# A decoder step on one core: cached values become the stationary operand of the probability products

## What is computed

```python
s = (jnp.einsum('bqhd,bqkhd->bhqk', qblk[:, :, g], kg) * scale
     - slopes[g][None, :, None, None] * dist.astype(jnp.float32)[None, None, None, :])
s = jnp.where(valid[None, None], s, NEG_INF)
lse = jax.nn.logsumexp(s, axis=-1)
p = jnp.exp(s - lse[..., None])
outs.append(jnp.einsum('bhqk,bqkhd->bqhd', p, vg))
...
wts = jax.nn.softmax(jnp.stack(lses, axis=0), axis=0)
return jnp.einsum('gbhq,gbqhd->bqhd', wts, jnp.stack(outs, axis=0))
```

## Time and profile before

| what | value |
|---|---|
| median of 3 runs | 940.0 us (938.59 to 940.89) |
| the profiled execution's own time | 937.09 us |
| its span on the core | 935.0 us |
| mean granted PE clock | 0.992 |
| PE busy (with its weight loads: PEld) | 905.9 us, 97% (840.2 us, 90%) |
| DVE, ACT, POOL busy | 556.4, 322.9, 209.7 us |
| stage B, by the trace | from about 405 to 702 us |

### The profile page before, as it was taken

How to read it: one execution, slowest core, us unless ns; L and a number is a source line. 1 busy time by engine, 2 the same in 40 slices (tenths; PEclk the granted TensorE clock), 3 DMA queues, 4 the chain that set the end, 5 groups by cost and what they waited for, 6 DMA issues and landing times.

```text
span 935.0 us, 19353 instructions
## 1 busy us (share of the span) xinstructions
PE 905.9 (97%) x6844; PEld 840.2 (90%) x6844; DVE 556.4 (60%) x1013; ACT 322.9 (35%) x512; POOL 209.7 (22%) x179
## 2 busy tenths in 40 slices
PE   7999999999999999999999999999989999999996
PEld 6998999999999999997887877877759999999996
DVE  4348634863476347656876786786787333333377
ACT  4134403440344034344544453453455222222210
POOL 0037202720272027241123114115110000000003
PEclk8999999999999999999999999999999999999999
DMA  7999799689968996573783693694596978888712
GB/s 214 215 271 325 290 183 268 235 295 181 280 220 294 181 270 233 208 249 110 265 313 132 228 355 123 204 349 154 191 367 210 302 256 262 267 270 286 233 63 102
DMA packets 163819, 221.04 MB, mean 236 GB/s; under 512 B 9088, under 2 KB 136832, under 8 KB 162048
## 3 DMA queue, kind: packets, MB, share of 16 engines
q1 hardware_dynamic: 158944, 207.09, 71.5%
q0 software_dynamic: 4176, 11.02, 3.6%
q10 hardware_dynamic: 656, 2.36, 0.7%
HBM read 207.71 MB, written 100.01 MB: 329 GB/s over the span
## 4 chain that ended last, share of the span: by engine, by line
PE 80%; DVE 10%; issue 4%; DMA 2%; ACT 2%; POOL 0%; DVEq 0%; SPq 0%; POOLq 0%; ACTq 0%
PE bank L757 19%; PE bank L759 19%; PE bank L758 19%; PE bank L1056 6%; PE bank L752 5%; PE bank L787 4%; PE bank L882 2%; DVE wl L1505 2%; PE bank L1101 2%; PE bank L1092 2%; PE bank L1018 1%; DMA xn<-in_x_prompt_dram 1%; DVE part_l L1734 1%; PE bank L1115 1%; PE bank L857 1%
## 5 line engine op out<-in xcount | busy, mean ns | idle before, releaser
L757 PE MATMUL bank<-xh,wh 128*128 128x288 f32 x640 | 191.8, 300 | 3.2 <-DVE vn L1572 3.1
L759 PE MATMUL bank<-xh,wl 128*128 128x288 f32 x640 | 188.7, 295 | 0.0
L758 PE MATMUL bank<-xl,wh 128*128 128x288 f32 x640 | 188.6, 295 | 0.0
L757 PE MATMUL bank<-wh,xh 128*128 128x256 f32 x640 | 184.7, 289 | 0.7 <-DVE qk L1700 0.6
L758 PE MATMUL bank<-wl,xh 128*128 128x256 f32 x640 | 181.0, 283 | 0.0
L759 PE MATMUL bank<-wh,xl 128*128 128x256 f32 x640 | 180.9, 283 | 0.0
L1505 DVE TENSOR_TENSOR wl<-raw,wh 128x1024 fp32r<-128x1024 f32 (+1 forms) x104 | 130.2, 1286 | 14.3 <-ACT wh L1260 13.0
L1260 ACT ACTIVATE wh<-raw 128x1024 fp32r<-128x1024 f32 (+1 forms) x104 | 102.3, 1018 | 79.7 <-PE bank L787 42.2
L757 PEld LDWEIGHTS bank<-wh,xh 128*128 128x128 f32 x640 | 123.0, 192 | 2.5 <-DVE qk L1700 0.8
L757 PEld LDWEIGHTS bank<-xh,wh 128*128 128x128 f32 x640 | 120.2, 188 | 5.2 <-DVE vn L1572 2.6
L758 PEld LDWEIGHTS bank<-wl,xh 128*128 128x128 f32 x640 | 123.1, 192 | 0.6
(11 more groups left out here) (219 smaller groups left out, 1755.5 us busy)
## 6 DMA issues: line engine op xcount, KB each, us to landing
raw<-in_w_in_dram SPq DMA_DIRECT2D x128, 256.0 KB
cslot<-in_cache_kv_w_dram SPq DMA_DIRECT2D x32, 1024.0 KB, 5.9
out_dram<-in_cache_kv_w_dram SPq DMA_DIRECT2D x16, 2040.0 KB, 10.1
out_dram<-in_cache_kv_w_dram SPq DMA_DIRECT2D x32, 1020.0 KB, 10.0
far<-in_cache_kv_w_dram SPq DMA_DIRECT2D x32, 512.0 KB, 10.4
out_dram<-in_cache_kv_w_dram SPq DMA_DIRECT2D x20, 504.0 KB, 10.8
raw<-in_w_in_dram SPq DMA_DIRECT2D x16, 512.0 KB
out_dram<-in_cache_kv_w_dram SPq DMA_DIRECT2D x24, 252.0 KB, 3.1
```

What stands on the lines that cost most here:

```text
L757: pe.matmul(out, lhs[0](k), rhs[0](k), start=(k == 0), stop=False)
L758: pe.matmul(out, lhs[0](k), rhs[1](k), start=False, stop=False)
L759: last = pe.matmul(out, lhs[1](k), rhs[0](k), start=False, stop=(k == n - 1))
```

## The change

1. In `cached_output` the operands change places. For every tile and each of the 4 heads, the tile's 128 x 128 block of that head's values is stationary and 16 columns of `pm` move (8 queries, high and low part, as 2 x 8 with a step of 32): with `part_h` and `part_l` that is 8 matmuls a tile for 2. The output comes out turned: `bank[4]`, 128 rows (head dimension) x 64 columns.
2. ACT's `output_lows`, DVE's `output_sum` and PE's `cached_turn` go. DVE's `output(x)` waits for PE's last tile, copies the 32 low columns to a new tile `osum`, adds the 32 high ones, and multiplies into `oa`. PE waits for `co_read` ahead of the score tiles, not behind them, since they write the bank that `output` reads.
3. On DVE `statistics` of a body stands behind `probs(1)` and the first three value tiles; it stood ahead of `next_projected(0)`.
4. On DVE in stage A, `values(22)` stands ahead of `far_sum(2)`, `far_sum(3)` moves behind `output(1)`, and the later far sums each move back by one place.

```diff
+        osum = sb("osum", [P, ROWS], F32, scope_b)
...
                     pe.wait_ge(qm_done, r * 2 + (x + 1))
                     settle(pe)
+                    pe.wait_ge(co_read, r * 2 + (x + 1))
+                    settle(pe)
                     for j in range(KTILES):
                         if j + 2 < KTILES:
                             transpose_tile(r, x, j + 2)
                         score_tile(j)
-                    pe.wait_ge(co_read, r * 2 + (x + 1))
-                    settle(pe)
...
                         n, probs = (P, pm[:, i * BLK:(i + 1) * BLK]) if i < TILES else (OWN, pn[:, :])
-                        for part in (part_h, part_l):
-                            last = pe.matmul(bank[4][0:BLK, :], probs, part[i % 3][0:n, :],
-                                             start=(i == 0 and part is part_h), stop=(i == TILES and part is part_l))
+                        for h in range(H):
+                            o, q = (a.rearrange("p (s h q) -> p s h q", s=2, h=H)[:, :, h, :] for a in (bank[4][:, 0:BLK], probs))
+                            for part in (part_h, part_l):
+                                last = pe.matmul(o, part[i % 3][0:n, h * DH:(h + 1) * DH], q,
+                                                 start=(i == 0 and h == 0 and part is part_h),
+                                                 stop=(i == TILES and h == H - 1 and part is part_l))
                         last.then_inc(part_used, 1)
-
-                def cached_turn(x):
-                    pe.wait_ge(co_sum, r * 2 + (x + 1))
-                    settle(pe)
-                    for h in range(H):
-                        last = turn(bank[5][:, 384 + h * ROWS:384 + (h + 1) * ROWS], srow[:, h * DH:(h + 1) * DH])
-                    last.then_inc(ct_done, 1)
...
-                def output_lows(x):
-
-                    act.wait_ge(part_used, r * (2 * PARTS) + (PARTS * x + PARTS + 1))
-                    act.activation(srow[:, 0:512], bank[4][ROWS:BLK, :], ACT.Copy).then_inc(co_lows, 1)
...
                 softmax(2)
                 values(21)
                 probs(1, 5)
+                values(22)
                 far_sum(2)
-                values(22)
-                far_sum(3)
                 softmax(3)
                 output(0)
                 zr(0)
                 probs(2, 7)
                 output(1)
-                far_sum(4)
+                far_sum(3)
                 low(c + 6, 0)
                 zr(1)
                 probs(3, 9)
                 output(2)
+                far_sum(4)
                 far_sum(5)
-                far_sum(6)
                 zr(2)
                 output(3)
+                far_sum(6)
                 far_sum(7)
...
-                def output_sum(x):
-                    dve.wait_ge(co_lows, r * 2 + (x + 1))
-                    tt(srow[:, 0:512], bank[4][0:ROWS, :], srow[:, 0:512], ALU.add).then_inc(co_sum, 1)
-
                 def output(x):
 
-                    dve.wait_ge(ct_done, r * 2 + (x + 1))
+                    dve.wait_ge(part_used, r * (2 * PARTS) + (PARTS * x + PARTS + 1))
+                    own.after(dve.tensor_copy(osum[:, :], bank[4][:, ROWS:BLK]))
+                    own.after(tt(osum[:, :], bank[4][:, 0:ROWS], osum[:, :], ALU.add))
                     o = oav[:, :, bass.ds(r * 16 + 8 * x, DEC_T)]
-                    b = bank[5][:, 384:385]
-                    b = bass.AP(tensor=b.tensor, offset=b.offset, ap=[b.ap[0], [ROWS + DEC_T, H], [1, DEC_T]])
+                    b = osum[:, :].rearrange("p (h q) -> p h q", h=H)
                     tt(o, b, o, ALU.mult).then_inc(co_read, 1)
...
                 rows(1)
                 normalise_rows(1)
-                statistics()
                 next_projected(0)
                 probs(1)
                 lows(1, 1, 0, 3)
+                statistics()
                 next_projected(1)
```

## The result

The changed kernel takes 1041.0 us (median of 4 runs, 1035.8 to 1046.3), the kernel before 939.3 us (938.1 to 940.9). The ratio is 1.110, 95% interval 1.107 to 1.114: 101.7 us slower, where +28 was forecast. The time lies in the stated range and within 2 us of the rival in which the clock falls. (A ratio leaves out each kernel's profiled execution and single executions over 1.5% above its fastest, so it can differ a little from the ratio of the medians.)

The account below looks back on a forecast made before the run. PE, busy 97% of the span, was taken as the bound. Terms 37.1 + 2 - 2.8 - 1.0 - 3.6 - 3.4 = +28.3 us on 937.1 gave 965.4, with 2.9 for the median 968 us; range 957 to 1052.

Parts of the forecast that it names:

- 8 x 0.11 = 0.88 us a tile: Stage B value tiles: eight loads at 0.11 us each, more than DVE's 0.64, make PE the bound in every tile.
- rival 1: Stage B: few moving columns let PE's clock fall despite busy loads; +75 us, 1043 us (1010 to 1070); chance 0.40.
- Pair of load and matmul, 0.11 us, 12.8 us a batch, +5.3: Stage B: matmul hides behind its load; 14 tiles plus group entries take 12.8 us against 7.5; seven batches +37.1.
- Last batch, +2: Last batch of stage B: first DVE wait goes, tiles stretch, statistics fall uncovered between third and fourth tile; +2 us (0 to +4).
- Turned output: Behind batches: PE's `srow` turns go, -2.8 us over seven; shorter chain to stage C behind the last, -1.0 us.
- Statistics moved, -3.6: Ahead of second batches in stage B: PE's 1.20 us wait for `part_l` goes, -1.2 x 3 = -3.6 us.
- What is late next is `normalise`: Stage B after the statistics' move: six value tiles and two `low` pieces still stand ahead of it on DVE, costing nothing.
- Far sums moved, -3.4: Stage A: `values(22)` ahead of `far_sum(2)` spares PE waits for `vn` in four heads, -3.4 us (0 to -4.5).
- no `vn` wait in stage A: Sign expected in the profile: PE in stage A no longer waits for DVE's `vn`; no separate size given.
- Once before the end: Clock of the kernel before: one granted-clock drop, at 695.5 us, behind six 512-column matmuls and a 1.53 us wait.
- Rival 2: Value tiles: a 128-column load costs only about 0.06 us, 0.5 us a tile, giving 929 us; chance 0.05.
- rival 3: Value tiles: load and matmul times add up, +24 us over the forecast, 992 us; chance 0.07.

Follow-up runs that it names:

- 128-column kernel: The changed kernel with each matmul streaming its 16 columns eight times over, same loads and number of matmuls: 970.5 us, ratio 1.032.
- 16-column kernel: The changed kernel itself, each matmul moving 16 columns, against the kernel before: 1041.0 us, ratio 1.110.
- 968.9-us kernel: 128-column kernel with the last batch's statistics spread one by one over value tiles 3 to 7 and `normalise` behind its last tile: 968.9 us, ratio 1.0325.
- the one with 64 columns: The changed kernel with each matmul streaming its 16 columns four times over, same loads and number of matmuls: 1007.0 us, ratio 1.065.
- the exchange alone: The changed kernel with both moves of DVE's order (statistics, far sums) taken back: 1062.4 us, ratio 1.131.

## Why the prediction was wrong

**The step that failed** is the price "8 x 0.11 = 0.88 us a tile", a load's time at the full clock, put for every tile and so for the work between them. The clock's fall stood beside it as a rival at 0.40 and not in the sum. That PE is the bound in every tile was right. But the clock fell, by rival 1's mechanism: few columns move, and busy loads don't hold it up. A pair took 0.21 us where it had fallen, stage B ran some 160 us at 1.2 GHz (3.4 before), and 70.5 of the 101.7 us came back with 128 columns for each load. The prediction said that no row of the trace before could decide this, and the runs with 64 and 128 columns decide it. That the time lies near the rival's 1043 us and not the forecast's 968 means that the forecast was wrong; the range held because it took the rival in.

Point by point:

- *Pair of load and matmul, 0.11 us, 12.8 us a batch, +5.3*: right. 0.11 us apart, and +5.6 and +4.6 us for a first and a second batch at full clock. The group entries are six and not five, which is 0.1 us.
- *The whole sum without the clock's fall, 968 us*: the 128-column kernel takes 970.5, but that it comes so near is luck. With both moves taken back it is 47.6 us slower than the kernel before, where the sum has +35.3 for the exchange (the last batch alone is 11 us longer in the profile, where +2 was put), and the moves then give 15.3 where it has 7.0. Two errors of 12 and 8 us cancel in part.
- *Last batch, +2*: wrong in size by the same cause. 24.6 us for 13.2, at a clock of 0.55. Both named causes were there, the stretched tiles and the statistics' gap, but the clock was not in the term.
- *Turned output*: DVE's three instructions take 0.19 us each, as priced, and `co_read` costs PE no wait:

```profile
557.13 0.19 DVE L1773 COPY osum<-bank 128x32 f32<-128x32 f32 x1 [2.52 <-PE bank L1058]
557.36 0.19 DVE L1774 TENSOR_TENSOR osum<-bank,osum 128x32 f32<-128x32 f32 x1
557.68 0.19 DVE L1777 TENSOR_TENSOR oa<-osum,oa 128x32 f32 x1
```

  No run takes this part alone, so its -2.8 and -1.0 are not tested.
- *Statistics moved, -3.6; "What is late next is `normalise`", "so nothing"*: wrong for the operands as they were (+2.6 by the medians, +1.8 in PE's waits), since the weight chunk's transfer was late next. The step had looked at DVE's and POOL's order and not at when the chunk lands. With PE slowed by its loads the transfers have time, and there PE's waits ahead of second batches are gone (1.20 us in each of three with the moves taken back).
- *Far sums moved, -3.4*: right, -3.5 on the kernel before. The "no `vn` wait in stage A" was nearly so: 1.0 us in the changed kernel, 3.1 before.
- *Rival 1*, +75 for the clock over the forecast: the 16-column kernel is 70.5 us slower than the one with 128, and 73 over the forecast. The estimate of three quarters of 101 us was of the right size. Its "Once before the end" leaves out a fall at the start: in the kernel before the clock is also 0.50 from 9.4 to 16.2 us, behind 3.3 us in which PE was busy for 1.81 and waited for its inputs (the 8 in the earlier trace rows). That fall, too, came behind waits.
- *Rival 2*, cheap loads, and *rival 3*, load and matmul added up: both out, by 0.11 us a pair, with 16 columns and with 128.

By the Trainium skill ("TensorE: Matmul & The Clock Gate", Part 1) the gate follows how busy PE is. The runs here add that busy loads are not enough: they were busy 2.90 of 3.30 us ahead of a fall.

What was there to be seen beforehand? The fall at 695.5 us in the kernel before followed 3072 columns in six matmuls, and the new tiles would move 500 in such a time. The prediction wrote both numbers down and then held the gap to be the better sign. Six times fewer columns was the stronger one.

## What to carry to other kernels

Count two things when operands are exchanged: the weight loads, which set PE's pace here (0.11 us a pair, with 16 columns moving and with 128), and the columns that still move, since a stretch of loads with few columns can put the whole engine to 1.2 GHz, neighbours included (0.50 from 526.2 to 529.6 us, behind tiles of 16 columns, while matmuls of 256 ran). If so few columns can't be avoided, streaming them again beside the load cost nothing here and saved 70 us (128 for 16); but the form in which 512 columns move against 64 stationary ones was better than either, 938 us for 970. A wait taken away on one engine wants a look at the transfers that were landing during it.

## What was not expected of the hardware

- Weight loads do not hold the clock up: it fell behind 3.3 us in which PE had no gap and PEld was busy 88% of the time.
- The clock does not come back as easily as it stays: with 128 columns for each load, batches that began at the full clock kept it (1.00 over 24.9 and 21.1 us), and in the last batch, where it had fallen around a wait of 1.10 us, it stayed at 1.2 GHz for 24 us, to 3 us behind the batch, with the same loads and columns. The same batch without that wait stayed at 1.00 for 15 us (968.9-us kernel).
- The columns of a matmul cost nothing beside its load of 128: pairs with 16 and with 128 columns both stand 0.11 us apart.
- Kernels whose clock falls often in stage B spread more from run to run: a standard deviation of 4.3, 7.0 and 5.3 us for the changed kernel, the one with 64 columns and the exchange alone, four runs each, against 2.2 over 17 runs of the kernel before.
